# Gate products of a PEER expert layer: packed for TensorE, made by VectorE and ScalarE, without GpSimd's transposing copy

## What is computed

```
q = (xb @ w_q).reshape(PEER_BLOCK, PEER_HEADS, 2, PEER_D_KEY // 2)
s = jnp.einsum('thcd,cnd->thcn', q, sub_keys)
s1, i1 = lax.top_k(s[:, :, 0], 16);  s2, i2 = lax.top_k(s[:, :, 1], 16)
cand_s = s1[..., :, None] + s2[..., None, :]      # 256 candidates of each head
top_s, top_pos = lax.top_k(cand_s, 16)            # 16 experts of 128 * 128, named by two keys
gate = jax.nn.softmax(top_s, axis=-1)
act = jax.nn.gelu(jnp.einsum('thkd,td->thk', u_tab[experts], xb))
y = jnp.einsum('thk,thkd->td', gate * act, v_tab[experts])
```

## Time and profile before

| what | value |
|---|---|
| median of 3 runs | 3272.99 us (3272.36 to 3275.35) |
| the profiled execution, its own time | 3266.96 us |
| its span | 3265.2 us |
| TensorE busy | 2851.1 us, 87% |
| VectorE busy | 1882.5 us, 58% |
| ScalarE busy | 1119.7 us, 34% |
| GpSimd busy | 282.0 us, 9% |
| granted TensorE clock, mean of the span | 0.924 |

### The profile page before, as it was taken

How to read it: one execution, slowest core, us unless ns; L and a number is a source line. 1 busy time by engine, 2 the same in 40 slices (tenths; PEclk the granted TensorE clock), 3 DMA queues, 4 the chain that set the end, 5 groups by cost and what they waited for, 6 DMA issues and landing times.

```text
span 3265.2 us, 60101 instructions
## 1 busy us (share of the span) xinstructions
PE 2851.1 (87%) x22131; PEld 2596.3 (80%) x22131; DVE 1882.5 (58%) x3520; ACT 1119.7 (34%) x2050; POOL 282.0 (9%) x377
## 2 busy tenths in 40 slices
PE   6845667999999999997569999976799999999998
PEld 5634555899999999996348888861589999999998
DVE  2265553698889655541533444452169888955554
ACT  1222210244444444441123444430024444444443
POOL 0013210000111000000001111112000011100000
PEclk9968977999999999998768999996799999999999
DMA  4300001354444455554001222225245444445554
GB/s 151 116 18 21 15 9 55 119 181 153 143 143 147 156 180 180 181 188 167 0 1 41 58 58 58 58 62 150 83 131 181 149 145 145 143 162 181 181 181 139
DMA packets 112351, 377.98 MB, mean 116 GB/s; under 512 B 14569, under 2 KB 24042, under 8 KB 111538
## 3 DMA queue, kind: packets, MB, share of 16 engines
q1 hardware_dynamic: 88562, 322.17, 29.5%
q0 software_dynamic: 13248, 43.98, 4.5%
q10 hardware_dynamic: 10368, 9.44, 1.0%
HBM read 371.52 MB, written 4.01 MB: 115 GB/s over the span
## 4 chain that ended last, share of the span: by engine, by line
PE 71%; issue 15%; DVE 9%; ACT 2%; DMA 1%; ACTq 1%; DVEq 0%; SPq 0%; POOLq 0%; POOL 0%
PE ps L709 69%; DVE arena L1215 3%; ACT arena L1836 2%; DVE arena L1219 1%; DMA arena<-in_cache_n 1%; PE ps L959 1%; PE ps L746 1%; DVE arena L1599 1%; DVE arena L1590 1%; ACTq L529 1%; DVE arena L1229 0%; ACTq L530 0%; DVE ring_lo L1215 0%; DVE arena L1594 0%; PE ps L965 0%
## 5 line engine op out<-in xcount | busy, mean ns | idle before, releaser
L1215 DVE TENSOR_TENSOR ring_lo<-ring,w_hi 128x1024 fp32r<-128x1024 f32 x512 | 625.8, 1225 | 457.5 <-ACT w_hi L1836 451.7
L1836 ACT ACTIVATE arena<-ps 128x264 f32<-128x264 f32 (+18 forms) x1021 | 413.7, 424 | 1249.9 <-PE ps L709 1083.6
L709 PE MATMUL ps<-arena 64*64 64x64 f32 (+11 forms) x5228 | 570.1, 297 | 187.2 <-DVEq L1212 62.2
L709 PEld LDWEIGHTS ps<-arena 64*64 64x64 f32 (+6 forms) x5228 | 444.0, 166 | 303.6 <-issue 74.2
L1836 ACT ACTIVATE w_hi<-ring 128x1024 fp32r<-128x1024 f32 x512 | 541.8, 1059 | 390.6 <-PE ps L709 390.2
L709 PE MATMUL ps<-x_hi,w_hi 128*128 128x264 f32 x2048 | 595.0, 291 | 15.5 <-DVE ring_lo L1215 15.5
L709 PE MATMUL ps<-h_hi,w_hi 128*128 128x264 f32 x2048 | 580.1, 283 | 6.8 <-DVE ring_lo L1215 6.8
L709 PE MATMUL ps<-x_lo,w_hi 128*128 128x264 f32 x2048 | 584.9, 286 | 0.0
L709 PE MATMUL ps<-x_hi,ring_lo 128*128 128x264 f32 x2048 | 583.8, 285 | 0.0
L709 PE MATMUL ps<-h_lo,w_hi 128*128 128x264 f32 x2048 | 582.3, 284 | 0.0
L709 PE MATMUL ps<-h_hi,ring_lo 128*128 128x264 f32 x2048 | 582.1, 284 | 0.0
(11 more groups left out here) (164 smaller groups left out, 2281.2 us busy)
## 6 DMA issues: line engine op xcount, KB each, us to landing
ring<-in_wstream SPq DMA_DIRECT2D x608, 512.0 KB, 3.3
arena<-in_cache_t POOLq DMA_DIRECT2D x128, 192.0 KB, 2.6
arena<-in_cache_n ACTq DMA_DIRECT2D x72, 128.0 KB, 2.7
arena<-in_cache_n POOLq DMA_DIRECT2D x56, 128.0 KB, 2.8
arena<-in_mla_w POOLq DMA_DIRECT2D x1, 3072.0 KB, 10.2
arena<-in_state POOLq DMA_DIRECT2D x4, 512.0 KB, 4.2
out_wkv_s<-arena POOLq DMA_DIRECT2D x4, 512.0 KB, 3.9
arena<-in_consts SPq DMA_DIRECT2D x1, 1408.0 KB
```

Source lines behind the costliest of these rows:

```text
L709: return nc.tensor.matmul(out, lhsT, rhs, start=start, stop=stop, **kw)
L1215: return v.tensor_tensor(out, a, b, op)
L1836: return nc.scalar.activation(out, in_, func, **kw)
```

## The change

Both gate operands change their layout and their maker. `oh1` is used as the stationary operand as it is, with a step of four elements between its columns; the copy `oh1c` and GpSimd's `gate_rows` are gone. `oh2g` is laid out part, token, key (`[128, 2, 4, 128]`), so that the moving operand is packed. Its upper part is made by VectorE for the four tokens at once (512 elements, read key by token and written with a step of 128 elements between neighbours). Its lower part is made by ScalarE, with one activation for each token: a copy of `oh2[:, :, u]` (128 elements, read with a step of four) with the token's lower gate part as a scale per partition. That part (`low`) is kept in f32 and no longer cast. ScalarE's four activations stand behind `upper` in each turn, two sets ahead of TensorE; they wait for `oh2_made`. TensorE waits for `ohlow_made` in place of `oh1_ready`.

```diff
-        oh1c = [a[:, 2 * OHT * P:3 * OHT * P].rearrange("p (u n) -> p u n", u=OHT) for a in oh]
-        oh2g = [a[:, 3 * OHT * P:].rearrange("p (k n u) -> p k n u", k=2, u=OHT) for a in oh]
+        oh2g = [a[:, 2 * OHT * P:].rearrange("p (k u n) -> p k u n", k=2, u=OHT) for a in oh]
...
-            def gate_rows(layer):
-
-                for i in range(NSETS):
-                    pool.wait_ge(oh1_made, NSETS * layer + i + 1)
-                    nc.gpsimd.tensor_copy(oh1c[i % OHS], oh1[i % OHS].rearrange("p n u -> p u n")).then_inc(oh1_ready, 1)
...
-                    pe.wait_ge(oh1_ready, s0 + i + 1)
+                    pe.wait_ge(ohlow_made, s0 + i + 1)
                     pe.wait_ge(oh2g_made, s0 + i + 1)
                     for u in range(OHT):
                         for k in range(2):
-                            last = mm(ps[:, b, u * P:(u + 1) * P], oh1c[st][:, u, :], oh2g[st][:, k, :, u], k == 0, k == 1)
+                            last = mm(ps[:, b, u * P:(u + 1) * P], oh1[st][:, :, u], oh2g[st][:, k, u, :], k == 0, k == 1)
...
-                own(tt(rest, rest, idxh[:, 2, :], ALU.subtract))
-                own(v.tensor_copy(idxh[:, 3, :], rest))
+                tt(low, rest, idxh[:, 2, :], ALU.subtract).then_inc(low_ready, 1)
...
-                    tt(oh1[st], keys8, these(0, 1).broadcast_to([P, P, OHT]), ALU.is_equal).then_inc(oh1_made, 1)
+                    tt(oh1[st], keys8, these(0, 1).broadcast_to([P, P, OHT]), ALU.is_equal)
+                    if i >= OHS:
+                        dve.wait_ge(ohlow_made, s0 + i - OHS + 1)
                     tt(oh2[st], keys8, these(1, 1).broadcast_to([P, P, OHT]), ALU.is_equal).then_inc(oh2_made, 1)
                     dve.wait_ge(oh2_made, s0 + i + 1)
-                    tt(oh2g[st], oh2[st].unsqueeze(1).broadcast_to([P, 2, P, OHT]),
-                       these(2, 2).unsqueeze(2).broadcast_to([P, 2, P, OHT]), ALU.mult).then_inc(oh2g_made, 1)
+                    tt(oh2g[st][:, 0].rearrange("p u n -> p n u"), oh2[st],
+                       these(2, 1).broadcast_to([P, P, OHT]), ALU.mult).then_inc(oh2g_made, 1)
...
+                def gate_low(i):
+
+                    st = i % OHS
+                    act.wait_ge(oh2_made, s0 + i + 1)
+                    if i >= OHS:
+                        act.wait_ge(oh_used, s0 + i - OHS + 1)
+                    for u in range(OHT):
+                        last = fn(oh2g[st][:, 1, u, :], oh2[st][:, :, u], scale=low[:, i * OHT + u:i * OHT + u + 1])
+                    last.then_inc(ohlow_made, 1)
...
                         upper(n + WHI)
+                        if g * GROUP_S + k + OHS < NSETS:
+                            gate_low(g * GROUP_S + k + OHS)
```

More of the change, by code:

```diff
@@ L180, in build @@
         OH_AT = W_AT + WHI * D
-        oh_words = OHT * 5 * P // 2
+        oh_words = OHT * 4 * P // 2
         KEY_AT = OH_AT + 2560
@@ L316, in build @@
         oh2 = [a[:, OHT * P:2 * OHT * P].rearrange("p (n u) -> p n u", u=OHT) for a in oh]
-        oh1c = [a[:, 2 * OHT * P:3 * OHT * P].rearrange("p (u n) -> p u n", u=OHT) for a in oh]
-        oh2g = [a[:, 3 * OHT * P:].rearrange("p (k n u) -> p k n u", k=2, u=OHT) for a in oh]
+        oh2g = [a[:, 2 * OHT * P:].rearrange("p (k u n) -> p k u n", k=2, u=OHT) for a in oh]
         idx_at = KEY_AT + OHT * P // 2
         keys8 = arena[:, KEY_AT:idx_at].bitcast(F16).rearrange("p (n u) -> p n u", u=OHT)
-        idxh = arena[:, idx_at:idx_at + 5 * T // 2].bitcast(F16).rearrange("p (k t) -> p k t", t=T)
+        idxh = arena[:, idx_at:idx_at + 3 * T // 2].bitcast(F16).rearrange("p (k t) -> p k t", t=T)
+        low = arena[:, idx_at + 3 * T // 2:idx_at + 5 * T // 2]
         hpart = arena[:, ARENA - 2 * T:ARENA].rearrange("p (g t) -> p g t", g=2)
@@ L472, in build @@
         sel_ready = sem("sel_ready")
-        oh1_ready = sem("oh1_ready")
         oh_used = sem("oh_used")
-        oh1_made = sem("oh1_made")
         oh2_made = sem("oh2_made")
         oh2g_made = sem("oh2g_made")
+        ohlow_made = sem("ohlow_made")
+        low_ready = sem("low_ready")
         xhi_ready = sem("xhi_ready")
@@ L655, in _ @@
             pool.wait_ge(st_out, 64)
-            gate_rows(0)
             pool.wait_ge(x_added, 2)
@@ L681, in _ @@
                     page(pool, cache_n, it * NSLOT + n, cpN[n], natp_in[n])
-            gate_rows(1)
             pool.wait_ge(x_added, 4)
@@ L1925, in peer @@
                     upper(n + WHI)
+                    if n == TURN_AT + 1:
+                        act.wait_ge(low_ready, layer + 1)
+                    if 0 < n - TURN_AT <= OHS:
+                        gate_low(n - TURN_AT - 1)
                 for g in range(NGROUP):
```

## The result

The kernel became slower. Its median is 3370.84 us (3365.66 to 3378.3, 4 runs) against 3272.68 us (3266.22 to 3275.35, 4 runs) for the kernel before: a ratio of 1.0305, 95% interval 1.0279 to 1.033, some 98 us more. My forecast was 3220, with 3207 to 3260 as the range.

The account below looks back on a forecast made before the run. TensorE was taken to bound the gate stages. Packing its moving operand saves 55 us, less some 2 us for the last groups, 53 in all: median 3272.99 to 3220 us, range 3207 to 3260 (0.80), own range 3210 to 3229.

Parts of the forecast that it names:

- What bounds the kernel: Gate stage of both expert layers: TensorE, busy 60 of 60 us, sets the time; other engines matter only past that.
- Moving operand packed: TensorE's gate matmuls: 63 ns each in place of 115, saving 0.42 us a set, 55 us for 132 sets.
- Weights stepped: TensorE's gate weight loads at a step of 8 bytes: nothing lost, 30 ns of streaming under 54 ns of matmul.
- A: Gate matmuls: packing gives nothing or stepped weights take it back; saving 5 us, 3268 us; chance 0.10.
- C: Gate weight loads: stepped, they double the f32 pace to 0.22 us; 111 us more, 3384; chance 0.10 together with table loads.
- GpSimd's copy gone: 132 copies of 777 ns in the gate stages: dropping them gives nothing by itself.
- VectorE: the step that failed: VectorE's upper-part product of 512 elements: 0.69 us, between 0.42 and 1.22; 22.4 us a group against TensorE's 23.4, hidden closely.
- Rival B: Gate stage: VectorE becomes the bound if its product costs 1.22 us; 12 to 17 us lost, 3232 to 3237; chance 0.14.
- ScalarE: Its four lower-part products a set: about 0.28 us each, 1.12 a set, hidden even at 1.6.
- D: ScalarE: table loads of 1283 ns between gelu and scaled copies; over 190 us more; chance 0.10 together with slow weight loads.
- The sum: Whole kernel: 55 us saved less some 2 us for the last groups, 53; median 3220 us.

Follow-up runs that it names:

- packed-write run: Changed kernel with VectorE's upper-part product walked token by token, output packed and input read at a step of four: 3223.66 us, ratio 0.9857 to the kernel before.
- p2_steps: Changed kernel with matmuls and VectorE products at various steps added behind its end; total time says nothing; moving operand 56 ns packed, 116 at a step of 4.

## Why the prediction was wrong

- **What bounds the kernel.** Right for before (60 of 60 us), and after packing as long as VectorE keeps up (60 of 60 us in the packed-write run). In the changed kernel it doesn't.
- **Moving operand packed.** Right. Within a set the matmuls start 56 ns apart instead of 63, but a group of six sets and seven tiles takes 23.6 us in the packed-write run against 25.9, so a set saves 0.38 us where 0.42 was forecast. The stepped operand was what cost 115 ns, as argued from the 292-ns record; p2_steps shows it by itself. The Trainium skill's cacheline rule (SBUF — State Buffer, the note on cachelines), by which a step of 8 bytes is free, is contradicted for the moving operand: 116 ns against 56.
- **Weights stepped.** Right: 114 ns loads, and some 2 ns a matmul lost with a packed moving operand. Rivals A and C fall.
- **GpSimd's copy gone.** Nothing, as said, but with a part that I overlooked: beside it, it slowed VectorE's product by 0.33 us a set. That row of 1019 ns was thus no clean price.
- **VectorE: the step that failed.** The bound "above: 1.22 us, the 1024-element f32 row, if each element costs two" was none. The product written with a step of 128 elements took 2.48 us in place and 2.43 alone, twice the bound and 3.5 times the 0.69 us that I took. None of the rows that I read had an output that hops, and I bounded it by rows of packed outputs, which say nothing about it. The 0.69 is what the product costs when its output is packed and its input is read at a step of four. It isn't the longer hop alone: written at a step of four the product takes 1.31 us, which already passes both the bound and the 0.85 us from which VectorE decides.
- **Rival B.** Its mechanism is what happened. Its sum, with 2.18 us in the turn, gives groups of 28.0 to 31.5 us, measured 29.1 to 31.8 from the second on. I priced the product at 1.22 us in it, so that it ended at 3237, or at 1.4 by the page below, near 3250; no case of mine had 2 us for the product. The Trainium skill's figure for one-element hops of an output (Vector Engine (DVE) Microarchitecture Reference, 5.2) is for 4-byte words; its 1.71 ns a column for long hops agrees with the f32 row here (1032 ns less the 0.14 us of start, over 512: 1.74), while f16 elements cost 4.5 ns by the same sum.
- **ScalarE.** Right in place and close in size: 399 ns each, four in 1.32 us instead of 1.12 + 0.10, hidden in the packed-write run; no table loads more (19 as before), so D falls.
- **The sum.** With the failed term put right by the other direction of the walk, the time is 3223.66 us on a chip whose before is 3270.08: 46 us saved of the 53 forecast. In the traces the two stages give 2 x 25.2 = 50 of it, against 55 for the moving operand less 2 for the last groups; these lost nothing, as their 23.6 us are those of the first. The few us between 50 and 46 lie outside the gate stages and aren't explained.

## What to carry to other kernels

A layout change moves a stride from a reader to a writer. Before making it, price the stride at each engine that would carry it: here a step of 8 bytes cost TensorE 60 ns for 128 columns, a hop of 128 elements cost VectorE's f16 write 2.0 us for 512 elements and a step of four 0.9 us, and the step of four on VectorE's read side cost 0.27 us. Where no row of the trace has the form, bound its cost by a form that shares its suspect property, or give the range a wide tail.

A transpose between two layouts of two-byte elements on VectorE should, by these rows, walk in the order of its output. An engine that stands close under the bound can take a good deal more work before it costs much: 35 us more of it a layer made TensorE's stage 4.0 us longer.

## What the runs showed of the hardware

- VectorE, product of 512 f16 elements by output step: 426 ns packed, 728, 1020, 1310, 1884, 2422 ns at 2, 3, 4, 6, 8 elements, 2335 at 16, 2432 at 128. It grows with the step up to 16 bytes and then no more. Why 2-byte elements cost 4.5 ns where 4-byte ones cost 1.7, and why pairs are free, stays open.
- TensorE, 128 f16 moving columns: 56, 58, 89, 116, 227 ns at steps of 1, 2, 3, 4, 8 elements; the 227 are the same at a granted clock of 1.00 and of 0.50. Weights at steps up to 8 cost 0 to 6 ns.
- GpSimd's copy of 512 elements beside it took VectorE's 1024-element product from 692 to 1019 ns, while the comparisons stayed at 416.
